# Down products with the activations stationary, and down weights staged a round ahead and copied by ScalarE, in a two-layer hybrid decoder trunk on one Trainium2 core

## The chip, the core and the metric

The kernel runs on one core of a Trainium2 chip. All times are microseconds (us) of device time for one execution, unless marked ns. The engines are TensorE (PE: matrix products; PEld is its weight load), VectorE (DVE), ScalarE (ACT), GpSimd (POOL) and SyncE (SP), whose queue here issues all loads from memory. Lower time is better.

## The reference

The program is a trunk of two residual layers on 256 tokens of width 1024, all in float32. Each layer has three token mixers (a gated delta rule, an RWKV-7 mixer and stick-breaking attention), which are merged by gates and projected. Layer 0 then has a dense SwiGLU of width 2816, layer 1 a mixture of 8 experts of width 3584 of which each token uses two. The mixture is what most of the change touches:

```
def swiglu(h, w_gate, w_up, w_down):
    return (jax.nn.silu(h @ w_gate) * (h @ w_up)) @ w_down

def moe_swiglu(h, router_w, w_gate, w_up, w_down):
    logits = (tokens @ router_w).astype(jnp.float32)
    top_vals, top_idx = lax.top_k(logits, TOP_K)
    top_w = jax.nn.softmax(top_vals, axis=-1)
    combine = jnp.sum(jax.nn.one_hot(top_idx, N_EXPERTS) * top_w[..., None], axis=1)
    for e in range(N_EXPERTS):
        y = swiglu(tokens, w_gate[e], w_up[e], w_down[e])
        out = out + combine[:, e:e + 1] * y
```

Reshapes and the token mixers are left out here.

## The kernel before, in words

Every engine runs its own program in its own order. They meet at semaphores: an instruction adds to one, another engine waits for a value. Nothing is scheduled by a planner; the order is that of the code.

**The expert stage** (`experts` on TensorE and VectorE, the loop at the end of the ScalarE program, and the loads at the end of the SyncE program) works in passes. A pass takes one expert and up to CAP = 80 of its tokens; there are eight passes in the profiled run. At its end a pass gathers the 80 tokens of the next one into xgT (products of the normed activations with a selection matrix). It then has NR = 4 rounds of FB = 7 tiles of 128 hidden columns each. A round on TensorE is:

- `hidden()`: gate and up products. The weights of the round lie in eight hidden slots (2 x 896 columns each). The weight tile is the stationary operand and the 80 tokens are the moving one. `columns_mm` splits each 128-column stationary tile in two halves of 64 columns, which write to the two halves of the output partitions. A semaphore (hid_used) frees each slot as soon as its products are done.
- ScalarE takes silu of the gate part (L1584 for four tiles, L1587 for three), VectorE multiplies with the up part into heT (128 hidden rows x 80 tokens for each of the 7 tiles).
- `down(0)` and `down(1)`: the products with the down weights, for the first four and the last three tiles. Again the weights are stationary, in halves of 64 columns, and heT moves; the result yT, 1024 outputs x 80 tokens, is summed in two banks of PSUM over all four rounds. The down weights of a round lie in three down slots (two, two and three tiles), freed by dwn_used (after `down(0)`) and dwn_mm.

At the end of a pass ScalarE copies yT out of PSUM (L1592), TensorE transposes it to 80 tokens x 1024 (L1292), ScalarE copies it again (L1596), and TensorE scatters it to all 256 tokens with the weighted selection matrix (L1299); VectorE adds that to x (L2032).

SyncE loads the eight hidden slots and then the three down slots of the following round, each after the semaphore that frees it. One hidden slot is 896 KB, the down slots are 1024, 1024 and 1536 KB. The first round's weights are loaded before the stage begins.

**Other places that the change touches.** At the start of each layer VectorE scales the activations of both token halves (`scaled`) and writes them transposed (`turned`) for TensorE's first products (L636). In `attention`, TensorE fills the waits between the attention products with pieces of the gate projections (`some(steps, 5)`, each piece being 2 products); a projection writes to one of two banks, and can only begin when VectorE has copied the one before last out of its bank (`opened`, L1876). In the dense SwiGLU the last three down tiles are kept back and done for one half of the tokens after the other.

The two lines of the code below that matter most are the products of `down` before:

```
ins = columns_mm(B[4 + half], slice(k % 4 * CAP, (k % 4 + 1) * CAP),
                 down_slot(n)[:, at, k * P:(k + 1) * P], heT[:, f, :], start=False, stop=False)
```

The functions that the change touches, with the line numbers of the profile:

Of the kernel before, what the change touches and what calls it, by code (L numbers as in the profile page):

```python
# [12 lines left out]
P = 128  # L13
D = 1024
# [5 lines left out]
DEPTH = 2  # L20
# [47 lines left out]
def build(nc, a, out):  # L68
    ctx = ExitStack()
    with ctx:  # L70
# [41 lines left out]
        eps_c = sb("eps_c", [P, 4])  # L112
        zeros = sb("zeros", [P, 4 * CAP], mybir.dt.bfloat16)
        stat = sb("stat", [P, 64])
# [19 lines left out]

        def down_slot(n):

            lo = 2 * KH * HSLOT
            return pool[:, lo + 2 * n * D:lo + min(2 * n + (3 if n == 2 else 2), FB) * D].rearrange("p (f n) -> p f n", n=D)

        assert 2 * KH * HSLOT + FB * D <= MRING * SLOT  # L140

# [80 lines left out]
        heT = region(FB * CAP).rearrange("p (j n) -> p j n", j=FB)  # L222
        yT = region(KD * CAP).rearrange("p (k n) -> p k n", k=KD)
        sge = region(FB * CAP).rearrange("p (j n) -> p j n", j=FB)
# [212 lines left out]
        he_silu, he_ready, hid_mm, dwn_mm = ff_silu.handle, ff_ready.handle, proj_mm.handle, down_mm.handle  # L437
        yT_ready = sem("yT_ready")
        ye_mm = sem("ye_mm")
        ye_ready = sem("ye_ready")  # L440
# [152 lines left out]
        def _(pe):  # L593
# [422 lines left out]
            def attention(l, steps):  # L1016
# [79 lines left out]
            def dense_ffn(l):  # L1096
# [39 lines left out]
                for c, (g, u, d) in list(enumerate(L[l]["ffn"]))[1:]:  # L1136
                    arrived(g)
                    arrived(u)
                    for i in range(2):
                        f = 2 * c + i  # L1140
                        ff_ready.wait(pe, 0, f - 1)
                        for s, w in ((0, weights(g)), (1, weights(u))):
                            for k in range(KD):
                                ins = mm(proj[f % 2][:, s * T:(s + 1) * T], w[:, k, i * P:(i + 1) * P], hnT[:, k, :],  # L1144
                                         start=(k == 0), stop=(k == KD - 1))
                        ff_mm.by(ins)

# [62 lines left out]
            def experts():  # L1210
# [7 lines left out]
                with pe.Fori(0, n_pass) as i:  # L1218
                    pe.wait_ge(xg_ready, i * 2 + 2)
                    pe.wait_ge(selT_ready, i + 1)  # L1220
                    for half in range(2):
                        mm(B[4 + half][:, 0:4 * CAP], zeros[:, 0:P], zeros[:, :], start=True, stop=False,
                           skip_group_check=True)
                    with pe.Fori(0, NR) as j:
# [38 lines left out]
                        def down(g):  # L1263

                            pe.wait_ge(he_ready, i * (2 * NR) + j * 2 + (ff_base + g + 3))
                            for f in groups[g]:
                                n, at = min(f // 2, 2), f - 2 * min(f // 2, 2)
                                if at == 0:
                                    pe.wait_ge(dwn_loaded[n],
                                               i * (16 * NR) + j * 16 + 16 * (slot_count[2 * KH + n] + 1))  # L1270
# [55 lines left out]
        def _(act):  # L1326
# [238 lines left out]
            for l in range(DEPTH):  # L1565
# [14 lines left out]
            n_pass = act.value_load(pass_expert[0:1, 0:1], min_val=MIN_PASSES, max_val=MAX_PASSES)  # L1580
            with act.Fori(0, n_pass) as i:
                for r in range(NR):
# [24 lines left out]
        def _(v):  # L1607
# [299 lines left out]
            def dense_ffn(l):  # L1907
# [3 lines left out]
                for t in range(NT):  # L1911
                    down_mm.wait(v, 0, down_mm.per_layer - 2 * (1 - t))
                    for half in range(2):
# [147 lines left out]
        def _(sp_):  # L2061
# [51 lines left out]
            def down_load(n, e, rows):  # L2113

                src = a["moe_w_down"][0, e, rows, :].rearrange("a (f p) n -> p (a f) n", p=P)
                sp_.dma_start(down_slot(n), src).then_inc(dwn_loaded[n], 16)  # L2116

# [12 lines left out]
            for ring in [None] + sorted(range(RING), key=lambda n: slot_last[n]):  # L2130
# [8 lines left out]
            assert len(fetched) == 2 * KH  # L2139

            sp_.wait_ge(passes_ready, 1)
            sp_.dma_start(fgain, a["final_norm_g"].partition_broadcast(P)).then_inc(fgain_loaded, 16)

            def later_round(e, col, hid, dwn):

                for n in range(2 * KH):
                    sp_.wait_ge(hid_used, hid + (n + 1))
                    hidden_load(n, bass.ds(e, 1), bass.ds(col, FB * P))
                for n in range(3):
                    if n < 2:  # L2150
                        sp_.wait_ge(dwn_used, dwn + 1)
                    else:
                        sp_.wait_ge(dwn_mm, dwn * 2 + (down_base + 2))
                    lo, size = down_rows(n)
                    down_load(n, bass.ds(e, 1), bass.ds(col + lo, size))

            def rest_of_pass(i, e):

                with sp_.Fori(0, NR - 1) as j:
                    later_round(e, j * (FB * P) + FB * P, i * (2 * KH * NR) + j * (2 * KH), i * NR + j)  # L2160

            more = sp_.value_load(pass_expert[0:1, MAX_PASSES + 1:MAX_PASSES + 2], min_val=MIN_PASSES - 1,
                                  max_val=MAX_PASSES - 1)
            with sp_.Fori(0, more) as i:
                e = sp_.value_load(pass_expert[0:1, bass.ds(i + 1, 1)], min_val=0, max_val=NE - 1)
                rest_of_pass(i, e)
                e = sp_.value_load(pass_expert[0:1, bass.ds(i + 2, 1)], min_val=0, max_val=NE - 1)
                later_round(e, 0, i * (2 * KH * NR) + (2 * KH * (NR - 1)), i * NR + (NR - 1))
            e = sp_.value_load(pass_expert[0:1, bass.ds(more + 1, 1)], min_val=0, max_val=NE - 1)
            rest_of_pass(more, e)  # L2170
            sp_.wait_ge(fin_ready, 1)
# [32 lines left out]
```

## Time and profile before

| what | value |
|---|---|
| median of three runs | 2055.0 us (2054.35 to 2058.61) |
| the profiled execution's own time | 2054.16 us |
| its span (first to last instruction) | 2052.4 us |
| TensorE busy | 1962.2 us (96%) |
| VectorE, ScalarE, GpSimd busy | 392.6, 271.1, 88.2 us |
| expert stage, from 1182 us to 2043 us | 861 us, TensorE busy 819.75 us, memory reads at 397 GB/s |
| dense SwiGLU, from 470 us to 696 us | 226 us, TensorE busy 225.66 us, 134 GB/s |
| mean granted TensorE clock, as a share of full speed | 0.984 |

The span lies 1.8 us under the time of its own execution, and that execution 0.8 us under the median. Busy time of TensorE is an upper bound on its work: products are pipelined, and their ends are modelled. A float32 product appears as two records (a MATMUL row with x64 stands for 32 products).

### The profile page before, as it was taken

Reading aid. Unit: us, or ns where it says so; the run is one execution under the profiler, and the core shown is the slowest. Engines: PE = TensorE matmul, PEld = TensorE weight load, DVE = VectorE, ACT = ScalarE, POOL = GpSimd, SP = SyncE. Lnnn points to the kernel's source line nnn. Section 1 sums busy time; section 2 is a strip of 40 time slices with the busy share of each in tenths; the row PEclk is TensorE's granted clock in tenths of the full one; section 3 lists DMA queues with packets and bytes.
Section 4 is the critical chain, followed back from the end, with each engine's and each line's share of the span. In section 5 each row is a group of like instructions: output and inputs, shape, how many; then the busy total and the mean of one; then the engine's idle time right before and its main releaser. Section 6 shows DMA issues by size and latency. Waiting matters only on the chain.

```text
span 2052.4 us, 66808 instructions
## 1 busy us (share of the span) xinstructions
PE 1962.2 (96%) x31214; PEld 1742.7 (85%) x31214; DVE 392.6 (19%) x948; ACT 271.1 (13%) x579; POOL 88.2 (4%) x174
## 2 busy tenths in 40 slices
PE   7999999999999999999999799999999999999997
PEld 7888887888777788888788799999999898989896
DVE  3335331110000133533211300101000101010001
ACT  1223223000000122222320000000000000000001
POOL 4011101000000001011000000000000000000000
PEclk9999999999999999999999899999999999999999
DMA  7313123467442151311345389999999999999996
GB/s 239 123 44 102 43 84 103 144 207 244 144 144 82 42 160 47 101 45 43 107 139 204 137 335 407 407 407 407 407 407 407 407 407 407 407 407 407 407 407 240
DMA packets 214760, 482.92 MB, mean 235 GB/s; under 512 B 11582, under 2 KB 110092, under 8 KB 214668
## 3 DMA queue, kind: packets, MB, share of 16 engines
q1 hardware_dynamic: 214668, 481.54, 62.9%
q8 instruction: 77, 1.26, 0.3%
q14 instruction: 15, 0.12, 0.0%
HBM read 480.46 MB, written 1.05 MB: 235 GB/s over the span
## 4 chain that ended last, share of the span: by engine, by line
PE 83%; DMA 6%; SPq 4%; DVE 3%; ACT 1%; issue 1%; POOL 0%; DVEq 0%; POOLq 0%
PE bank L1190 29%; PE bank L623 18%; PE bank L1144 7%; DMA pool<-in_moe_w_down_dram 6%; PE bank L713 5%; PE bank L1071 4%; PE bank L1104 4%; SPq L2111 3%; PE bank L1087 3%; PE bank L636 2%; PE bank L677 2%; PE bank L1299 1%; SPq L2116 1%; PE bank L1034 1%; DVE pool L1814 0%
## 5 line engine op out<-in xcount | busy, mean ns | idle before, releaser
L1190 PE MATMUL bank<-pool 128*64 128x80 f32 x21504 | 759.5, 234 | 32.1 <-DMA pool<-in_moe_w_down_dram 23.5
L1190 PEld LDWEIGHTS bank<-pool 128*64 128x64 f32 x21504 | 752.6, 138 | 40.3 <-DMA pool<-in_moe_w_down_dram 25.8
L623 PE MATMUL bank<-hnT,pool 128*128 128x256 f32 x1856 | 431.5, 386 | 6.4 <-DVE pool L1876 6.4
L623 PEld LDWEIGHTS bank<-hnT,pool 128*128 128x128 f32 x1856 | 349.0, 192 | 61.7 <-issue 14.4
L1144 PEld LDWEIGHTS bank<-hnT,pool 128*128 128x128 f32 x640 | 121.6, 190 | 24.6 <-issue 9.1
L1144 PE MATMUL bank<-hnT,pool 128*128 128x256 f32 x640 | 141.2, 379 | 0.0
L2019 DVE TENSOR_TENSOR pool<-pool,bank 128x320 f32<-128x320 f32 x32 | 15.6, 488 | 637.4 <-ACT pool L1584 637.4
L713 PEld LDWEIGHTS bank<-pool 64*64 64x64 f32 x3008 | 94.8, 135 | 17.2 <-issue 11.3
L713 PE MATMUL bank<-pool 64*64 64x32 f32 (+2 forms) x3008 | 103.4, 221 | 2.6 <-DVE pool L1660 1.6
L1584 ACT ACTIVATE pool<-bank 128x320 f32<-128x320 f32 x32 | 14.0, 437 | 675.5 <-PE bank L1190 675.5
L561 POOL TENSOR_TENSOR pool<-pool,level_mask 128x256 f32<-128x256 f32 x72 | 51.9, 736 | 782.1 <-DVE pool L1736 502.1
L1071 PE MATMUL bank<-oT,pool 128*128 128x256 f32 x384 | 85.4, 380 | 0.0
L1071 PEld LDWEIGHTS bank<-oT,pool 128*128 128x128 f32 x384 | 72.8, 190 | 10.2 <-issue 0.3
L1104 PE MATMUL bank<-pool 128*128 128x512 f32 x176 | 78.8, 592 | 0.0
L1104 PEld LDWEIGHTS bank<-pool 128*128 128x128 f32 x176 | 33.4, 190 | 33.5 <-issue 27.7
L1087 PE MATMUL bank<-pool 128*128 128x256 f32 x256 | 55.9, 379 | 0.0
L1087 PEld LDWEIGHTS bank<-pool 128*128 128x128 f32 x256 | 48.5, 190 | 6.5
L636 PE MATMUL bank<-hnT,pool 128*128 128x128 f32 x384 | 47.9, 290 | 4.6 <-DVE hnT L1631 4.6
L636 PEld LDWEIGHTS bank<-hnT,pool 128*128 128x128 f32 x384 | 47.3, 206 | 5.1 <-issue 5.0
L1910 DVE TENSOR_TENSOR pool<-pool,bank 128x256 f32<-128x256 f32 x22 | 9.3, 421 | 204.8 <-ACT pool L1562 204.8
L1660 DVE TENSOR_TENSOR pool<-pool,bank 128x128 f32<-128x128 f32 x108 | 26.7, 285 | 92.5 <-PE bank L713 92.5
L1562 ACT ACTIVATE pool<-bank 128x256 f32<-128x256 f32 x22 | 8.4, 383 | 206.8 <-PE bank L1144 195.7
(323 smaller groups left out, 1222.4 us busy)
## 6 DMA issues: line engine op xcount, KB each, us to landing
pool<-in_moe_w_up_dram SPq DMA_DIRECT2D x128, 896.0 KB, 16.6
pool<-in_moe_w_gate_dram SPq DMA_DIRECT2D x128, 896.0 KB, 16.6
pool<-in_w_in_dram SPq DMA_DIRECT2D x66, 1024.0 KB, 5.3
pool<-in_moe_w_down_dram SPq DMA_DIRECT2D x64, 1024.0 KB, 16.8
pool<-in_moe_w_down_dram SPq DMA_DIRECT2D x32, 1536.0 KB, 18.6
pool<-in_ffn_w_gate_dram SPq DMA_DIRECT2D x11, 1024.0 KB, 8.5
pool<-in_ffn_w_up_dram SPq DMA_DIRECT2D x11, 1024.0 KB, 5.7
pool<-in_ffn_w_down_dram SPq DMA_DIRECT2D x11, 1024.0 KB, 5.1
```

Of the source, the lines that this page charges most:

```text
L561: ml_ready.by(gp.tensor_tensor(Ml[:, 4 * g:4 * g + 4, :], m_of(g), rep(level_mask[:, b, :], 4), ALU.mult))
L623: ins = mm(ps[:, s * T:(s + 1) * T], w[:, k, (j + s) * P:(j + s + 1) * P], hnT[:, k, :], start=(k == 0), stop=(k == KD - 1))
L636: ins = mm(ps[:, s * T + t * P:s * T + (t + 1) * P], w(s, k), hnT[:, k, t * P:(t + 1) * P], start=(k == 0), stop=(k == KD - 1))
L677: ins = mm(ps[:, half * SW:(half + 1) * SW], hnT[:, k, t * P:(t + 1) * P], weights(n)[:, k, :], start=(k == 0), stop=(k == KD - 1))
L713: ins = mm(out(rows), lhs(rows), rhs(rows), start=True, stop=True, skip_group_check=True)
L1071: ins = mm(ps[:, s * T:(s + 1) * T], weights(n)[:, k, (j0 + s) * P:(j0 + s + 1) * P], oT[:, m // 4, k, :], start=(k == 0), stop=(k == GH - 1))
L1087: ins = mm(bank[:, s * SW:(s + 1) * SW], mT[:, k, t * P:(t + 1) * P], weights(n)[:, k, :], start=(k == 0), stop=(k == KD - 1))
L1104: ins = mm(B[2 * t + half][:, :], ffT[:, f, t * P:(t + 1) * P], weights(n)[:, i, half * 512:half * 512 + 512], start=(f == 0), stop=(f == ...
L1144: ins = mm(proj[f % 2][:, s * T:(s + 1) * T], w[:, k, i * P:(i + 1) * P], hnT[:, k, :], start=(k == 0), stop=(k == KD - 1))
L1190: ins = mm(bank[rows, cs], w[:, rows], rhs, start=start, stop=stop, skip_group_check=True)
L1660: ins = tt(old, old, part(B[2 + g][:, k * T:(k + 1) * T]), ALU.subtract)
L2111: sp_.dma_start(hidden_slot(n), src).then_inc(hid_loaded[n], 16)
```

## The change

It has one large part, in the expert stage, and three small ones.

1. **Down products.** heT (128 x 80) becomes the stationary operand and the down weights move, 512 columns at a time. The result is 80 tokens x 1024 outputs, so the transposes at the end of a pass and one of the two copies go away. `columns_mm` is not used for them any more.
2. **Down weights.** SyncE loads them into a stage (copy 0) a round ahead, ScalarE copies them from the stage into the slots that TensorE reads (copy 1). The stage takes the place of the former down slots, the slots are new. ScalarE's copies wait for the load and for TensorE's last read of the slot; SyncE's loads wait for ScalarE's copy.
3. **Small parts.** In `attention` TensorE's second filling has 4 pieces and not 5, and VectorE copies gate block 0 out after the first two heads and not after four. In the dense SwiGLU six down tiles are kept back and not three. At a layer's start VectorE writes the first half transposed before it scales the second.

```
@@ the stage and the slots
+        def down_tiles(n, copy):
+            lo = 2 * KH * HSLOT + copy * FB * D
+            return pool[:, lo + 2 * n * D:lo + min(2 * n + (3 if n == 2 else 2), FB) * D]
...
@@ TensorE, down(g)
-                                    for k in range(4 * half, 4 * half + 4):
-                                        ins = columns_mm(B[4 + half], slice(k % 4 * CAP, (k % 4 + 1) * CAP),
-                                                         down_slot(n)[:, at, k * P:(k + 1) * P], heT[:, f, :],
-                                                         start=False, stop=False)
+                                    ins = mm(B[4 + half][0:CAP, :], heT[:, f, :],
+                                             down_slot(n)[:, at, half * 512:half * 512 + 512], start=False, stop=False,
+                                             skip_group_check=True)
...
@@ TensorE, end of a pass
-                    for half in range(2):
-                        pe.wait_ge(yT_ready, i * 2 + (half + 1))
-                        for k in range(4):
-                            ins = pe.transpose(B[2 + half][0:CAP, k * P:(k + 1) * P], yT[:, 4 * half + k, :], ident[:])
-                        ins.then_inc(ye_mm, 1)
...
@@ ScalarE
+            def down_copy(n):
+                A(down_tiles(n, 1), down_tiles(n, 0), ACT.Copy).then_inc(dwn_ready, 1)
+
+            for n in range(3):
+                act.wait_ge(dwn_loaded[n], 16 * (slot_count[2 * KH + n] + 1))
+                down_copy(n)
...
+            def next_down(i, r, n):
+
+                act.wait_ge(dwn_loaded[n], i * (16 * NR) + 16 * (slot_count[2 * KH + n] + r + 2))
+                if n < 2:
+                    act.wait_ge(dwn_used, i * NR + (r + 1))
+                else:
+                    act.wait_ge(dwn_mm, i * (2 * NR) + (2 * r + down_base + 2))
+                down_copy(n)
...
+                    if not last or r < NR - 1:
+                        next_down(i, r, 0)
+                        next_down(i, r, 1)
+                        if r < NR - 1:
+                            next_down(i, r, 2)
...
-                    A(yT[:, 4 * half:4 * half + 4, :], B[4 + half][:, 0:4 * CAP].rearrange("p (k n) -> p k n", k=4),
-                      ACT.Copy).then_inc(yT_ready, 1)
-                for half in range(2):
-                    act.wait_ge(ye_mm, i * 2 + (half + 1))
-                    A(ye[0:CAP, half * 512:half * 512 + 512], B[2 + half][0:CAP, :], ACT.Copy).then_inc(ye_ready, 1)
+                    A(ye[0:CAP, half * 512:half * 512 + 512], B[4 + half][0:CAP, :], ACT.Copy).then_inc(ye_ready, 1)
+                if not last:
+                    next_down(i, NR - 1, 2)
...
@@ SyncE: in each round hidden slots of the next round, then the stage of the one after it
+            def down_round(i, r, e):
+
                 for n in range(3):
+                    sp_.wait_ge(dwn_ready, i * (3 * NR) + (3 * r + 3 + dwn_base + n + 1))
                     lo, size = down_rows(n)
+                    lo += (r + 2) % NR * FB * P
+                    down_load(n, e, slice(lo, lo + size))
...
@@ small parts
-                    some(steps, 5)
+                    some(steps, 4)
                     values(j)
...
-                opens = ((), (0, 1), (2,), (3,))
+                opens = ((0,), (1,), (2,), (3,))
...
-                        if f - 1 >= LAST - 2:
+                        if f - 1 >= LAST - 5:
...
+                v.wait_ge(vec_ready, l + 1)
+                turned(l, 0, 0)
                 scaled(l, 0, 1)
-                v.wait_ge(vec_ready, l + 1)
-                for t in range(NT):
-                    turned(l, 0, t)
+                turned(l, 0, 1)
```

How the order of instructions moves is shown at three places. The first is TensorE's round in the expert stage: the end of the hidden products and both down groups, before the change (one product is one row count here; L1190 is the line of `columns_mm`).

```order
L1190 MATMUL bank<-pool 64x80 x136
L1239 REGISTER_ALU
L1190 MATMUL bank<-pool 64x80 x56
L1265 REGISTER_ALU
L1269 REGISTER_ALU
L1190 MATMUL bank<-pool 64x80 x64
L1265 REGISTER_ALU
L1190 MATMUL bank<-pool 64x80 x48
L1224 REGISTER_ALU
```

And with the change (L1192 is `columns_mm`, L1275 the new product):

```order
L1192 MATMUL bank<-pool 64x80 x136
L1241 REGISTER_ALU
L1192 MATMUL bank<-pool 64x80 x56
L1267 REGISTER_ALU
L1271 ISA
L1271 REGISTER_ALU
L1275 MATMUL bank<-pool 80x512 x8
L1267 REGISTER_ALU
L1271 REGISTER_ALU
L1275 MATMUL bank<-pool 80x512 x6
```

The 64 + 48 down products of 64 output rows by 80 columns have become 8 + 6 of 80 rows by 512; the hidden products (32 more stand ahead of these rows) are as they were.

The second place is ScalarE between two rounds of a pass, before the change: the two silu of one round (L1584, L1587) and of the next.

```order
L1584 ACTIVATE pool<-bank 128x320
L1586 REGISTER_ALU
L1587 ACTIVATE pool<-bank 128x240
L1583 REGISTER_ALU
L1584 ACTIVATE pool<-bank 128x320
```

With the change (L1596, L1599 are the silu, L1573 the copies of the stage):

```order
L1596 ACTIVATE pool<-bank 128x320
L1598 REGISTER_ALU
L1599 ACTIVATE pool<-bank 128x240
L1586 REGISTER_ALU
L1588 REGISTER_ALU
L1573 ACTIVATE pool<-pool 128x2048 x2
L1590 REGISTER_ALU
L1573 ACTIVATE pool<-pool 128x3072
L1595 REGISTER_ALU
L1596 ACTIVATE pool<-bank 128x320
```

Three copies, of 2048, 2048 and 3072 elements a partition, now stand between the silu of one round and those of the next.

The third place is VectorE at the start of layer 0, before the change: L1625 is `scaled`, L2039 copies the vectors, L1631 is `turned` (two rows for each half of the tokens).

```order
L1625 TENSOR_SCALAR hn<-x,stat 128x1024
L2039 COPY vecs<-bank 128x103
L1625 TENSOR_SCALAR hn<-x,stat 128x1024
L1631 TENSOR_TENSOR hnT<-bank,vecs 128x4x128 x4
L1674 MEMSET pool 128x4x4
```

With the change (L1644, L2058 and L1650 are the same three):

```order
L1644 TENSOR_SCALAR hn<-x,stat 128x1024
L2058 COPY vecs<-bank 128x103
L1650 TENSOR_TENSOR hnT<-bank,vecs 128x4x128 x2
L1644 TENSOR_SCALAR hn<-x,stat 128x1024
L1650 TENSOR_TENSOR hnT<-bank,vecs 128x4x128 x2
```

The second `scaled` has moved behind the first half's two `turned` instructions.

## Rows read from the trace of the kernel before

**Rows 1.** Windows: length, PE, PEld, DVE, ACT, POOL busy, clock, DMA share, GB/s
```profile
480.00:685.00 205.00, 205.00 (x810) 152.14 (x810) 8.43 (x20) 7.66 (x20) 0.00 (x0) 1.00 0.38 126
1290.00:1398.00 108.00, 103.56 (x2779) 99.93 (x2777) 9.98 (x26) 6.46 (x13) 0.00 (x0) 0.98 1.03 407
```

**Rows 2.** Page, part 6: issues, KB each, us from issue to landing
```profile
pool<-in_moe_w_up_dram SPq DMA_DIRECT2D x128, 896.0 KB, 16.6
...
pool<-in_moe_w_down_dram SPq DMA_DIRECT2D x64, 1024.0 KB, 16.8
pool<-in_moe_w_down_dram SPq DMA_DIRECT2D x32, 1536.0 KB, 18.6
```

**Rows 3.** Waits from 1200 us to the end: us in total, times, longest
```profile
PE bank L1190 <- DMA pool<-in_moe_w_down_dram: 23.5, 14, 2.1
...
PE bank L1190 <- DMA pool<-in_moe_w_up_dram: 5.3, 6, 0.9
```

**Rows 4.** Windows: one round, from silu to silu
```profile
1224.09:1247.52 23.43, 23.43 (x679) 23.30 (x676) 3.24 (x13) 0.81 (x3) 0.00 (x0) 1.00 1.03 406
```

**Rows 5.** The chain that ended last, dense SwiGLU: start, us, what
```profile
492.33 3.43 PE bank L1104 x8
...
685.36 10.31 PE bank L1104 x24
```

**Rows 6.** Timeline at a pass's end: start, us, engine, operation, count, idle before
```profile
1280.04 2.39 PE L1190 MATMUL bank<-pool,hn 128*64 128x80 f32 x64
...
1282.36 1.07 PE L1292 MATMUL bank<-ident,pool 128*80 128x128 f32 x8
1282.47 0.49 DVE L2000 TENSOR_TENSOR pool<-bank,vecs 128x320 f32<-128x320 f32 x1 [0.61 <-PE bank L1190]
...
1283.77 3.67 PE L1299 MATMUL bank<-hnT,pool 80*128 80x512 f32 x8 [0.34 <-ACT hnT L1596]
...
1288.56 0.45 PE L1222 MATMUL bank<-zeros 128*128 128x320 bf16 x2 [0.89 <-DVE pool L2006]
...
1288.99 3.19 PE L1190 MATMUL bank<-pool 128*64 128x80 f32 x86
```

**Rows 7.** The chain, first pass of the expert stage
```profile
1182.64 9.49 PE bank L1190 x268
1192.13 0.21 issue
...
1196.99 1.83 issue
...
1208.49 0.67 issue
```

**Rows 8.** Timeline, attention of layer 0
```profile
308.60 0.56 DVE L1867 SCALAR_TENSOR_TENSOR pool<-bank,pool 128x384 f32<-128x384 f32 x1 [0.93 <-ACT pool L1531]
...
312.05 1.28 DVE L1876 COPY pool<-bank 128x512 f32<-128x512 f32 x2
...
312.88 1.19 PE L623 MATMUL bank<-hnT,pool 128*128 128x256 f32 x4 [3.20 <-DVE pool L1876]
```

**Rows 9.** Timeline, start of layer 1
```profile
699.23 0.74 DVE L1625 TENSOR_SCALAR hn<-x,stat 128x1024 f32<-128x1024 f32 x1
...
701.31 3.97 PE L636 MATMUL bank<-hnT,pool 128*128 128x128 f32 x17 [2.31 <-DVE hnT L1631]
```

**Rows 10.** Groups of ScalarE: count, busy, mean ns, idle before
```profile
L1405 ACT ACTIVATE pool<-pool 128x2048 f32<-128x2048 f32 x2 | 3.8, 1901 | 0.0
```

**Rows 11.** Timeline of ScalarE ahead of the expert stage
```profile
1159.24 0.20 ACT L1354 ACTIVATE stat<-stat 128x1 f32<-128x1 f32 x1
...
1169.47 0.20 ACT L1578 ACTIVATE pool<-pool 128x2 f32<-128x2 f32 x1 [10.03 <-DVE pool L1943]
```

**Rows 12.** Windows, ahead of the expert stage
```profile
1166.00:1170.00 4.00, 1.11 (x6) 1.01 (x6) 2.58 (x16) 0.20 (x1) 0.00 (x0) 0.50 0.00 0
```

**Rows 13.** Timeline, scatter of the last pass
```profile
2039.19 3.67 PE L1299 MATMUL bank<-hnT,pool 80*128 80x512 f32 x8 [0.34 <-ACT hnT L1596]
```

More of the change, by code:

```diff
@@ L112, in build @@
         eps_c = sb("eps_c", [P, 4])
-        zeros = sb("zeros", [P, 4 * CAP], mybir.dt.bfloat16)
+        zeros = sb("zeros", [P, 512], mybir.dt.bfloat16)
         stat = sb("stat", [P, 64])
@@ L133, in hidden_slot, with down_slot @@
             return pool[:, n * HSLOT:(n + 1) * HSLOT].rearrange("p (k n) -> p k n", k=2)
[L135 to L140, printed above, removed]
+        def down_tiles(n, copy):
+            lo = 2 * KH * HSLOT + copy * FB * D
+            return pool[:, lo + 2 * n * D:lo + min(2 * n + (3 if n == 2 else 2), FB) * D]
+        def down_slot(n, copy=1):
+            return down_tiles(n, copy).rearrange("p (f n) -> p f n", n=D)
+        assert 2 * KH * HSLOT + 2 * FB * D <= MRING * SLOT
         banks = [ctx.enter_context(nc.psum_tensor(f"bank{i}", [P, 512], F32)) for i in range(8)]
@@ L222, in build @@
         heT = region(FB * CAP).rearrange("p (j n) -> p j n", j=FB)
-        yT = region(KD * CAP).rearrange("p (k n) -> p k n", k=KD)
         sge = region(FB * CAP).rearrange("p (j n) -> p j n", j=FB)
@@ L437, in build @@
         he_silu, he_ready, hid_mm, dwn_mm = ff_silu.handle, ff_ready.handle, proj_mm.handle, down_mm.handle
-        yT_ready = sem("yT_ready")
-        ye_mm = sem("ye_mm")
+        dwn_ready, dwn_base = yrs_ready.handle, DEPTH * yrs_ready.per_layer
         ye_ready = sem("ye_ready")
@@ L1221, in experts @@
                     for half in range(2):
-                        mm(B[4 + half][:, 0:4 * CAP], zeros[:, 0:P], zeros[:, :], start=True, stop=False,
+                        mm(B[4 + half][0:CAP, :], zeros[:, 0:CAP], zeros[:, :], start=True, stop=False,
                            skip_group_check=True)
@@ L1268, in down @@
                                 if at == 0:
-                                    pe.wait_ge(dwn_loaded[n],
-                                               i * (16 * NR) + j * 16 + 16 * (slot_count[2 * KH + n] + 1))
+                                    pe.wait_ge(dwn_ready, i * (3 * NR) + j * 3 + (dwn_base + n + 1))
                             for half in range(2):
@@ L1579, in _, with one_pass @@
             act.wait_ge(passes_ready, 1)
-            n_pass = act.value_load(pass_expert[0:1, 0:1], min_val=MIN_PASSES, max_val=MAX_PASSES)
-            with act.Fori(0, n_pass) as i:
+            more = act.value_load(pass_expert[0:1, MAX_PASSES + 1:MAX_PASSES + 2], min_val=MIN_PASSES - 1,
+                                  max_val=MAX_PASSES - 1)
+            def next_down(i, r, n):
[5 more added lines that the diff above has]
+                down_copy(n)
+            def one_pass(i, last):
                 for r in range(NR):
@@ L1588, in _ @@
                       ACT.Silu).then_inc(he_silu, 1)
+                    if not last or r < NR - 1:
[3 more added lines that the diff above has]
+                            next_down(i, r, 2)
                 for half in range(2):
                     act.wait_ge(dwn_mm, i * (2 * NR) + (down_base + 2 * NR - 1 + half))
-                    A(yT[:, 4 * half:4 * half + 4, :], B[4 + half][:, 0:4 * CAP].rearrange("p (k n) -> p k n", k=4),
-                      ACT.Copy).then_inc(yT_ready, 1)
-                for half in range(2):
-                    act.wait_ge(ye_mm, i * 2 + (half + 1))
-                    A(ye[0:CAP, half * 512:half * 512 + 512], B[2 + half][0:CAP, :], ACT.Copy).then_inc(ye_ready, 1)
+                    A(ye[0:CAP, half * 512:half * 512 + 512], B[4 + half][0:CAP, :], ACT.Copy).then_inc(ye_ready, 1)
+                if not last:
+                    next_down(i, NR - 1, 2)
+            with act.Fori(0, more) as i:
+                one_pass(i, False)
+            one_pass(more, True)
             ln_exp_tables()
@@ L1911, in dense_ffn @@
                 for t in range(NT):
-                    down_mm.wait(v, 0, down_mm.per_layer - 2 * (1 - t))
+                    down_mm.wait(v, 0, down_mm.per_layer - 3 * (1 - t))
                     for half in range(2):
@@ L2115, in down_load @@
                 src = a["moe_w_down"][0, e, rows, :].rearrange("a (f p) n -> p (a f) n", p=P)
-                sp_.dma_start(down_slot(n), src).then_inc(dwn_loaded[n], 16)
+                sp_.dma_start(down_slot(n, 0), src).then_inc(dwn_loaded[n], 16)
             def down_rows(n):
@@ L2139, in _, with hidden_round @@
             assert len(fetched) == 2 * KH
+            for n in range(3):
+                sp_.wait_ge(dwn_ready, dwn_base + n + 1)
+                lo, size = down_rows(n)
+                down_load(n, slice(0, 1), slice(FB * P + lo, FB * P + lo + size))
             sp_.wait_ge(passes_ready, 1)
             sp_.dma_start(fgain, a["final_norm_g"].partition_broadcast(P)).then_inc(fgain_loaded, 16)
-            def later_round(e, col, hid, dwn):
+            def hidden_round(i, r, e):
+                col = (r + 1) % NR * FB * P
                 for n in range(2 * KH):
-                    sp_.wait_ge(hid_used, hid + (n + 1))
-                    hidden_load(n, bass.ds(e, 1), bass.ds(col, FB * P))
+                    sp_.wait_ge(hid_used, i * (2 * KH * NR) + (2 * KH * r + n + 1))
+                    hidden_load(n, e, slice(col, col + FB * P))
+            def down_round(i, r, e):
                 for n in range(3):
[L2150 to L2153, printed above, removed]
+                    sp_.wait_ge(dwn_ready, i * (3 * NR) + (3 * r + 3 + dwn_base + n + 1))
                     lo, size = down_rows(n)
[L2155 to L2160, printed above, removed]
+                    lo += (r + 2) % NR * FB * P
+                    down_load(n, e, slice(lo, lo + size))
             more = sp_.value_load(pass_expert[0:1, MAX_PASSES + 1:MAX_PASSES + 2], min_val=MIN_PASSES - 1,
@@ L2165, in _ @@
                 e = sp_.value_load(pass_expert[0:1, bass.ds(i + 1, 1)], min_val=0, max_val=NE - 1)
-                rest_of_pass(i, e)
+                e = bass.ds(e, 1)
+                for r in range(NR - 2):
+                    hidden_round(i, r, e)
+                    down_round(i, r, e)
+                hidden_round(i, NR - 2, e)
                 e = sp_.value_load(pass_expert[0:1, bass.ds(i + 2, 1)], min_val=0, max_val=NE - 1)
-                later_round(e, 0, i * (2 * KH * NR) + (2 * KH * (NR - 1)), i * NR + (NR - 1))
+                e = bass.ds(e, 1)
+                down_round(i, NR - 2, e)
+                hidden_round(i, NR - 1, e)
+                down_round(i, NR - 1, e)
             e = sp_.value_load(pass_expert[0:1, bass.ds(more + 1, 1)], min_val=0, max_val=NE - 1)
-            rest_of_pass(more, e)
+            e = bass.ds(e, 1)
+            hidden_round(more, 0, e)
+            down_round(more, 0, e)
+            hidden_round(more, 1, e)
+            hidden_round(more, 2, e)
+            down_round(more, 1, e)
             sp_.wait_ge(fin_ready, 1)
```

## The prediction, made before the changed kernel ran

> **What bounds the kernel now.** I read the windows by stage first. In the expert stage two limits lie close together: a pass takes 108 us, the memory reads run at 407 GB/s with the DMA engines' share at 1.03, and TensorE is busy for 103.56 of the 108 us [rows 1]. The sizes of the loads say which one binds: a round reads 8 x 896 + 2 x 1024 + 1536 KB = 11.01 MB [rows 2] (gate loads have the size of up loads), which at 407 GB/s is 27.05 us, so four rounds are 108.2 us. That is the pass. Before, memory sets the time of seven of the eight passes. The view of waits says how near TensorE is: it waits for down and up weights 23.5 + 5.3 = 28.8 us in the whole stage [rows 3], 3.6 us a pass. So TensorE has 3.6 us to spare in each pass and not more. That number decides the case, since the change alters the cost of a third of TensorE's products there.
>
> A round without waits takes TensorE 23.43 us [rows 4] for 224 hidden and 112 down products of 64 x 80, so 69.7 ns each: 15.62 us hidden, 7.81 us down.
>
> **The change part by part.**
>
> *Down products.* A round has 7 tiles x 2 halves = 14 products with 512 moving columns. The nearest row is the dense SwiGLU's, the same type and the same 512 columns, weights moving: 3.43 us for 4 products (8 records), 10.31 us for 12 [rows 5], so 0.859 us each, in a stretch where TensorE was busy for all of 205 us [rows 1]. 14 x 0.859 = 12.03 us in place of 7.81: **4.22 us more in each round**. Its stationary tile has 128 columns, the new one 80. From below: if the cost went by the filled output positions, 80 of 128, a product would cost 0.537 us and a round 7.5 us. From above stands the scatter: 4 products (8 records) of 512 columns over only 80 rows of the array took 3.67 us, 0.92 each [rows 6], with the last one's drain in it; 14 of those are 12.9 us, and the stage would take 27 us more than by 0.859. I take 0.859: the row that shares the length of the moving operand in an unbroken run. The scatter also speaks against the low value, since a part-filled array was not faster there.
>
> Why the old form was cheap can be read from the same rows: 69.7 ns for 80 columns in a 64-column half, two of which make the 128 columns of a tile, so 139 ns a tile, while 80/512 of 859 ns is 134 ns for a whole tile. The halves run side by side. The new form fills 80 of 128 output columns for its whole length. That is the loss: 128/80 = 1.6, less the small overhead of short products.
>
> The Trainium skill says this too, in TensorEngine Tiling, When to Use Tiling: swapping stationary and moving operand gains column tiling only where the operand that becomes stationary has a free size of at most 64. Here it has 80, so the swap gives up a tiling and gets none. The trace's 69.7 against 859 ns agrees, as far as the rows go.
>
> *The end of a pass.* Before, 1280.04 (gather) to 1288.99 (next round) is 8.95 us [rows 6]. The transposes L1292 and the first copy go; the scatter at 1283.77 then waits only for the second multiply of the gathered tokens, which ends at 1282.96 [rows 6], because the new copies of 80 x 512 run under the gather (the first half of the down sum is complete three products earlier, the second needs one copy, and the gather lasts 2.39 us). Scatter about 1283.07: 0.7 us gained. The zeroing product has 512 columns in place of 320, 0.45 us for two now [rows 6]: 0.2 us lost. 8.45 us.
>
> *A pass on TensorE* is 4 x (15.62 + 12.03) + 8.45 = **119.05 us**, over the 108.2 us that memory needs. TensorE becomes the limit, and the 28.8 us of waits vanish into it.
>
> *The stage and the copies.* A copy of 2048 elements a partition is 1.90 us on ScalarE [rows 10], one of 3072 by that 2.85, together 6.65 us a round; none is on the path. ScalarE idles more than 20 us of each round before (0.81 us busy of 23.43, [rows 4]). Copies 0 and 1 can begin when `down(0)` is done and end 3.8 us later, at about the end of `down(1)` (6 x 0.859 = 5.2 us); copy 2 ends 2.9 us into the next round, and the next silu comes after some 14 us of hidden products. What stands behind a waiting copy on ScalarE is that silu: if a stage load were late by more than about 11 us, TensorE would wait. It is not, as loads need 27.05 of a round's 27.65 us and catch up by 8.45 us at each pass's end. What was late before, the last down slot (freed only at the end of its round), is now hidden by the stage. But TensorE's wait for it was the 3.6 us spare, which is already counted.
>
> The first copies stand ahead of the exponential of the routing: ScalarE ends the norm at 1159.4 and is wanted at 1169.47 [rows 11], 6.65 us of copies fit. The loads of the first stage (9 us) go into a stretch where the DMA engines stand still [rows 12]; this helps a memory-bound stage and is worth nothing to one that TensorE binds.
>
> *Small parts.* In attention TensorE waits 3.20 us for VectorE's copy at 312.05 [rows 8]. The copy of block 0 alone can follow the multiply-add that ends at 309.16: TensorE resumes about 2.9 us earlier. The piece taken out of the second filling is done in the last filling, which has room for it, so it costs nothing. Twice, for two layers: 5.8 us. At a layer's start one `scaled` of 0.74 us leaves the path to L636 [rows 9]: 0.7 us a layer, 1.4. Six kept tiles and not three: the same products on the same engine, and VectorE's norm of the next layer still waits for both halves, so nothing. Together 7.2 us.
>
> **The sum**, against the profiled execution's 2054.2 us. Before, from the first product of the expert stage to the end of the last scatter: 1182.64 [rows 7] to 2042.86 [rows 13], 860.2 us. After: 8 x 119.05 = 952.4, less the 1.55 us of a pass's end that lie behind the scatter, plus the gaps of the first pass (four of them, 3.2 us in all; the first, the longest and the last are in [rows 7]) = 954.0 us. So +93.8 - 7.2 = +86.6: 2140.8 us for this execution; the median stands 0.8 us above it. I say **2140 us**, rounded down, since the first gaps may shrink when the loads come sooner.
>
> **Rivals.**
>
> *A, the other side: the long products are cheaper than the dense SwiGLU shows, and the stage stays bound by memory.* It decides at the product's price p where 4 x (15.62 + 14p) + 8.45 equals 108.2 us, p = 0.665 us; with the 7.2 us and the 9 us of early loads (2.0 us a pass) no loss remains up to 0.70 us. For p = 0.54, the low bound: 2054.2 - 7.2 - 9.0, plus about 2 us as the last load is followed by a copy before its products, = 2040 us. For it: only that no row shows 80 columns stationary with 128 rows. Against it: both rows with 512 moving columns lie at 0.86 to 0.92 us. Chance 0.04.
>
> The Trainium skill has a figure that would give this case: TensorE: Matmul & The Clock Gate, Back-to-back issue gap, gives about 131 ns for each 512-column product in a real stream, and about 216 ns for one by the simple formula. An estimate by that page, four times 131 ns for float32, is 0.52 us a product, and the stage would stay at the memory's pace. The trace is against it: 859 ns is four times 215 ns.
>
> *B: TensorE also waits, because the queues hold each other.* SyncE loads in one order: the third stage load waits for ScalarE's copy 2, which ends 2.9 us into the round, and the hidden loads stand behind it. If the DMA engines stood still for those 2.9 us in each round, a round would need 27.05 + 2.9 = 29.95 us and a pass 119.8, above 119.05: 8 x 0.8 = 6 us more; with a second wait of the same size for `down(0)`'s end, 8 x 3 = 24 us. For it: the copies, in-order queues, and a margin of only 0.6 us in a round. Against: hidden slots are only freed from some 3.6 us on, so the queue has work from before. 2146 to 2165 us, chance 0.09.
>
> *C: the small parts give nothing* (the attention is limited by ScalarE's chain right behind the wait): +7.2 us, 2147. It lies in the range and is part of the forecast's own chance.
>
> **How the numbers follow.** Forecast (TensorE-bound at 0.859 us a product) 0.85, its own range 2128 to 2150 (0.02 us a product is 14 x 32 x 0.02 = 9 us; small parts 0 to 8 us). A 0.04, B 0.09, and 0.02 for a price between. The range 2126 to 2158 leaves out A and the upper half of B, and of the high bound of 0.92 us (2167) it reaches two thirds. A measurement tells 0.2%, some 4 us, from no change: faster 0.03, within it 0.01, slower 0.96.
>
> **What would show it.** A new group with 512 columns, 448 products (896 records), near 385 us in all, in the place of a third of L1190's 759 us. Passes of 119 us at some 370 GB/s, no waits of TensorE for DMA, TensorE busy through. ScalarE with 96 copies, 1.9 and 2.9 us. The 3.2 us gap in the attention gone. I am wrong if the new products take 0.7 us or less, if passes stay at 108 us, or if TensorE waits for the copies.

## The result, and the profile after

The changed kernel takes **2143.2 us** (median of 4 runs, 2141.39 to 2144.91), the kernel before in the same comparison 2056.11 us. The ratio is 1.0423, with a 95% interval of 1.0404 to 1.0441: slower by 87 us, where 85 us were forecast (2140 against 2055). The profiled execution took 2144.91 us, where the prediction's sum gave 2140.8; its span is 2143.2 us.

The page's groups show where the time went. Columns as in part 5: line, engine, operation, tiles, count, busy us, mean ns, idle before and what ended it. L1192 is `columns_mm`, L1275 the new down product, L1573 ScalarE's copies. The first row is the same group in the kernel before.

```profile
L1190 PE MATMUL bank<-pool 128*64 128x80 f32 x21504 | 759.5, 234 | 32.1 <-DMA pool<-in_moe_w_down_dram 23.5
...
L1192 PE MATMUL bank<-pool 128*64 128x80 f32 x14336 | 503.3, 233 | 1.9 <-issue 1.9
...
L1275 PE MATMUL bank<-pool 128*80 128x512 f32 x896 | 391.8, 594 | 0.0
...
L1573 ACT ACTIVATE pool<-pool 128x2048 f32<-128x2048 f32 (+1 forms) x96 | 207.1, 2188 | 245.8 <-PE bank L1275 232.4
```

L1190's 759.5 us of before have become 503.3 + 391.8 = 895.1 us: 136 us more work for TensorE. The time rose by less, since in each pass some of the new work fills time in which TensorE waited for weights before [rows 3]. Now its idle time ahead of these products is 1.9 us in the whole stage, and none of it is for DMA. The chain that ended last shows a pass from the start of its rounds to the start of the next, in order of time (start us, us, what):

```profile
1297.18 15.64 PE bank L1192 x448
1312.83 12.17 PE bank L1275 x28
1325.00 15.64 PE bank L1192 x448
1340.64 12.17 PE bank L1275 x28
1352.82 15.64 PE bank L1192 x448
1368.46 12.17 PE bank L1275 x28
1380.64 15.65 PE bank L1192 x448
1396.28 12.17 PE bank L1275 x28
1408.46 2.39 PE bank L1192 x64
...
1411.49 3.71 PE bank L1294 x8
...
1416.92 3.12 PE bank L1192 x85
```

A round is 15.64 + 12.17 us without a gap, the end of a pass (gather at 1408.46 to the next round at 1416.92) 8.46 us, the pass 119.74 us. The windows of two passes answer to [rows 1] (length, busy time of PE, PEld, DVE, ACT, POOL, clock, DMA share, GB/s):

```profile
1297.00:1417.00 120.00, 118.44 (x1985) 82.93 (x1986) 9.97 (x26) 31.38 (x23) 0.00 (x0) 1.00 0.95 368
1417.00:1536.00 119.00, 117.47 (x1978) 82.48 (x1976) 9.97 (x26) 31.38 (x23) 0.00 (x0) 1.00 0.95 368
```

The memory reads have fallen from 407 to 368 GB/s: TensorE is now the slower of the two. Note how little PE's busy share tells: 96% in the window of before, 99% in these, and the limit has changed from one resource to the other.

### The profile page after: what moved, and what is told of

Read it like the earlier page. It is cut to its first block, busy times and chain, and to the rows that moved or that the text cites. A ratio compares the mean times of both kernels' runs of the same rounds, so it can differ in the third digit from the quotient of the medians.

```text
span 2143.2 us, 54280 instructions
## 1 busy us (share of the span) xinstructions
PE 2088.4 (97%) x24878; PEld 1615.0 (75%) x24878; DVE 392.5 (18%) x948; ACT 469.4 (22%) x658; POOL 88.4 (4%) x174
## 4 chain that ended last, share of the span: by engine, by line
PE 94%; DVE 3%; ACT 1%; issue 1%; DMA 0%; SPq 0%; POOL 0%; DVEq 0%
PE bank L1192 24%; PE bank L1275 18%; PE bank L625 18%; PE bank L1146 6%; PE bank L715 5%; PE bank L1073 4%; PE bank L1106 4%; PE bank L1089 3%; PE bank L638 2%; PE bank L679 1%; PE bank L1294 1%; PE bank L1036 0%; DVE pool L1833 0%; PE bank L770 0%; PE bank L996 0%
## 5 line engine op out<-in xcount | busy, mean ns | idle before, releaser
L1192 PEld LDWEIGHTS bank<-pool 128*64 128x64 f32 x14336 | 497.9, 137 | 24.6 <-issue 24.6
L1192 PE MATMUL bank<-pool 128*64 128x80 f32 x14336 | 503.3, 233 | 1.9 <-issue 1.9
L1275 PE MATMUL bank<-pool 128*80 128x512 f32 x896 | 391.8, 594 | 0.0
L625 PEld LDWEIGHTS bank<-hnT,pool 128*128 128x128 f32 x1856 | 349.5, 192 | 56.0 <-issue 8.5
L1275 PEld LDWEIGHTS bank<-pool 128*80 128x80 f32 x896 | 131.8, 150 | 235.2 <-issue 232.3
L1573 ACT ACTIVATE pool<-pool 128x2048 f32<-128x2048 f32 (+1 forms) x96 | 207.1, 2188 | 245.8 <-PE bank L1275 232.4
L1146 PEld LDWEIGHTS bank<-hnT,pool 128*128 128x128 f32 x640 | 121.6, 190 | 23.4 <-issue 7.6
L715 PEld LDWEIGHTS bank<-pool 64*64 64x64 f32 x3008 | 94.8, 135 | 17.3 <-issue 11.3
L1596 ACT ACTIVATE pool<-bank 128x320 f32<-128x320 f32 x32 | 14.0, 437 | 408.8 <-PE bank L1192 408.8
## 6 DMA issues: line engine op xcount, KB each, us to landing
pool<-in_moe_w_up_dram SPq DMA_DIRECT2D x128, 896.0 KB, 10.5
```

The source lines that it names most:

```text
L625: ins = mm(ps[:, s * T:(s + 1) * T], w[:, k, (j + s) * P:(j + s + 1) * P], hnT[:, k, :], start=(k == 0), stop=(k == KD - 1))
L715: ins = mm(out(rows), lhs(rows), rhs(rows), start=True, stop=True, skip_group_check=True)
L1192: ins = mm(bank[rows, cs], w[:, rows], rhs, start=start, stop=stop, skip_group_check=True)
L1275: ins = mm(B[4 + half][0:CAP, :], heT[:, f, :], down_slot(n)[:, at, half * 512:half * 512 + 512], start=False, stop=False, skip_group_chec ...
L1573: A(down_tiles(n, 1), down_tiles(n, 0), ACT.Copy).then_inc(dwn_ready, 1)
```

## The experiments

All times are medians, ratios against the kernel before on the same chip, with 95% intervals. The kernel before had a median of 2056.4 us beside experiments 1 to 4 and of 2055.8 us beside the others.

**1. The old products, with all the rest of the change.** In `down`, at the pass's end and in ScalarE's copies there:

```
-  ins = mm(B[4 + half][0:CAP, :], heT[:, f, :], down_slot(n)[:, at, half * 512:half * 512 + 512], ...)
+  for k in range(4 * half, 4 * half + 4):
+      ins = columns_mm(B[4 + half], slice(k % 4 * CAP, (k % 4 + 1) * CAP),
+                       down_slot(n)[:, at, k * P:(k + 1) * P], heT[:, f, :], ...)
```

> The changed kernel with one thing undone: the down products have the weights stationary again, in halves of 64 columns, with the transposes and both copies at a pass's end. The stage, ScalarE's copies, SyncE's order and the small parts stay. My theory (the long products alone make it slower, TensorE is the limit there): TensorE needs 4 x 23.44 + 8.95 = 102.7 us a pass, memory 108.2, so passes of 108 us again, the 9 us of early loads and the 7.5 us of the small parts show, and the time is 2036 to 2046 us, faster than before. Rival (ScalarE's copies and the queues that hold each other cost something of their own): TensorE waits for copies, 2056 us or more.

Measured: 2046.6 us, ratio 0.9952 (0.9935 to 0.9969). Undoing this one edit takes 96.6 us off and makes the kernel faster than before. So the long products alone are the loss. But it is 0.6 us above my range, and its median lies 4 us above that of experiment 3, which has no stage (the two intervals overlap). ScalarE's timeline in the last round shows a loss there, and experiment 7 tests it (start, duration, [idle before]):

```profile
2010.04 1.91 ACT L1582 ACTIVATE pool<-pool 128x2048 f32<-128x2048 f32 x1 [17.30 <-DMA pool<-in_moe_w_down_dram]
2012.51 1.91 ACT L1582 ACTIVATE pool<-pool 128x2048 f32<-128x2048 f32 x1 [0.56 <-DMA pool<-in_moe_w_down_dram]
2016.35 2.76 ACT L1582 ACTIVATE pool<-pool 128x3072 f32<-128x3072 f32 x1 [1.93 <-DMA pool<-in_moe_w_down_dram]
2019.02 0.42 ACT L1605 ACTIVATE pool<-bank 128x320 f32<-128x320 f32 x1
...
2020.25 10.01 PE L1195 MATMUL bank<-pool 128*64 128x80 f32 x224 [4.61 <-DVE pool L2051]
```

In the last pass the last stage loads stand behind all hidden loads, so they are not a round ahead any more: SyncE's code for that pass issues the hidden loads of the last two rounds and only then the last stage loads. ScalarE waits 17.3 us for them with the silu queued behind; TensorE waits 4.6 us and then needs 10.01 us for down products that took 7.8 us in the round of [rows 4]. The granted clock in the window from 2020 to 2025 us was 0.55, near the lower of the two levels, 1.2 GHz, after a stretch in which TensorE was mostly idle (0.64 of 5 us busy from 2015 to 2020 us).

**2. The new products without the stage.** The kernel before with the new `down`, the shorter pass end and the small parts; the loads go straight to the slots, ScalarE copies nothing.

> The kernel before with the new down products and the small parts, without the stage: loads go straight to the slots, ScalarE copies nothing. My theory: TensorE binds, so the stage is worth nothing to it, passes of 119.7 us, 2140 to 2146 us. Rival (the stage is what keeps the loads ahead, as a round has only 0.8 us more than its loads need): TensorE waits for the last down slot, some 2 us in each of 32 rounds, 2170 to 2210 us. Second rival (copies slow TensorE's products down): below 2135 us.

Measured: 2142.5 us, ratio 1.0419 (1.0401 to 1.0436), the same as the changed kernel. The chain shows the same rounds:

```profile
1415.91 15.64 PE bank L1188 x448
1431.55 12.17 PE bank L1272 x28
```

The stage and its 96 copies neither cost nor gain anything where TensorE binds. Both rivals of this run are out.

**3. The small parts alone**, on the kernel before:

```
-                    some(steps, 5)
+                    some(steps, 4)          # the second filling
-                opens = ((), (0, 1), (2,), (3,))
+                opens = ((0,), (1,), (2,), (3,))
```

with the six kept tiles and `turned` ahead of the second `scaled`, as in the diff above.

> The kernel before with the small parts alone: VectorE's earlier copy in attention, four pieces in the second filling, six down tiles kept back in the dense part, the first half written transposed before the second is scaled. My theory: 2.9 us a layer in attention and 0.7 us a layer at the start, 2048 to 2050 us. Rival (they only shift waits): 2054 to 2057 us.

Measured: 2042.4 us, ratio 0.9938 (0.9922 to 0.9955): 14 us faster by the medians, 9 to 16 us by the interval, where I had worked out 7.2. The two profiled executions lie 11.6 us apart (spans of 2040.8 and 2052.4 us). The chain of the attention in layer 0, from VectorE's copy on:

```profile
308.55 0.61 DVE pool L1876
309.16 0.14 issue
309.29 1.10 PE bank L623 x4
310.39 0.65 PE bank L1034 x2
311.04 0.22 PE bank L1035 x2
311.26 0.65 PE bank L1034 x2
```

and the same place in the kernel before:

```profile
312.13 0.61 DVE pool L1876
312.88 1.19 PE bank L623 x4
314.07 1.28 PE bank L1034 x2
315.35 0.43 PE bank L1035 x2
315.77 1.28 PE bank L1034 x2
```

After its wait of 3.2 us [rows 8] TensorE ran the same products in twice the time: each L1034 row, one product, took 1.28 us and not 0.65. The windows of before give the clock there:

```profile
312.00:314.00 2.00, 1.12 (x5) 1.01 (x6) 1.33 (x3) 0.00 (x0) 0.41 (x1) 0.94 1.02 388
314.00:316.00 2.00, 2.00 (x6) 1.30 (x5) 0.00 (x0) 0.19 (x1) 0.00 (x0) 0.50 0.01 3
316.00:318.00 2.00, 2.00 (x8) 1.41 (x7) 0.00 (x0) 0.79 (x2) 0.42 (x2) 0.71 0.00 0
```

The clock is 0.50 from 314 to 316 us, which is 1.2 GHz, after an idle stretch; without the wait it stays at 1.00. The wait cost 3.0 us by itself, the slow products 1.7 us, and some 0.3 us is left for the end of the attention, where TensorE no longer waits for the last chain of ScalarE and GpSimd: 5.0 us for this attention, where I had counted 2.9.

**4. 64 stationary columns, in pairs.** The down products leave out tokens 64 to 79 of each pass, and the second half of the outputs stays in the upper 64 partitions, where they are not copied out whole:

```
...
+  for half in range(2):
+      ins = mm(B[4 + half][64 * half:64 * half + 64, :], heT[:, f, 0:64],
+               down_slot(n)[:, at, half * 512:half * 512 + 512], ...)
```

> The changed kernel with 64 stationary columns in place of 80: the down products leave out tokens 64 to 79 of a pass, and the two output halves of a tile go to the two column halves of the array, one behind the other. The rest is as changed. If two 64-column products of 512 run side by side, a pair costs about 0.87 us, a round 6.1 us and TensorE needs 4 x 21.8 + 8.5 = 95.5 us a pass: bound by memory again, 2034 to 2046 us. If only the moving columns count and nothing runs side by side, it costs what 80 columns do: 2140 to 2146 us.

Measured: 2044.1 us, ratio 0.9938 (0.9921 to 0.9955). The same number of products with the same 512 moving columns:

```profile
L1275 PE MATMUL bank<-pool 128*64 128x512 f32 x896 | 200.4, 599 | 6.5 <-DVE pool L2038 6.5
```

200.4 us in place of 391.8, 0.895 us for a pair on average over the stage. The chain shows a round's down part in a pass:

```profile
1368.67 6.01 PE bank L1275 x28
```

That is 14 products in 6.01 us, 0.859 us for a pair, less than a single product of 80 columns takes (0.869). So two products run side by side in the two column halves. The stage is bound by memory again: the same part of the next pass begins at 1476.93, 108.3 us later, at 407 GB/s, and TensorE waits for gate and up weights. The form "activations stationary" is not dear in itself; 80 columns are: each of these products has TensorE for itself for 0.869 us and fills 80 of 128 columns. The 6.5 us of idle time in the row above are one wait in the last round, of the kind of experiment 1.

**5 and 6. Fewer moving columns.** The changed kernel with 448 and with 384 moving columns in each down product, which leaves out 128 and 256 of the 1024 outputs:

```
-  ins = mm(B[4 + half][0:CAP, :], heT[:, f, :], down_slot(n)[:, at, half * 512:half * 512 + 512], ...)
+  ins = mm(B[4 + half][0:CAP, 0:448], heT[:, f, :], down_slot(n)[:, at, half * 512:half * 512 + 448], ...)
```

> The changed kernel with 448 moving columns in each down product in place of 512 (it leaves out 128 of the 1024 outputs). All the rest is as changed. If the product's price goes by its moving columns, 0.869 x 448/512 = 0.760 us, a round is 15.64 + 10.65 us and a pass 4 x 26.29 + 8.46 = 113.6 us, still over the memory's 108.2: 8 x 6.1 us less than the changed kernel, 2094 us. If something else had set the 119.7 us, the time moves less than that.

> The same with 384 moving columns (it leaves out 256 of the 1024 outputs): 0.652 us a product, just under the 0.665 us at which the passes of TensorE and of memory are equal. A round is 24.77 us and a pass 107.5 us, so memory takes over at 108.2: 2050 to 2060 us with ScalarE's block in the last round, which cost the run with the old products some 7 us. If the price alone counted, without a floor, the next step from 448 columns would be as large as the last; memory's floor takes about 0.7 us of it in each pass.

Measured: 2095.1 us (ratio 1.0196, 1.0177 to 1.0214) and 2047.5 us (0.9958, 0.9943 to 0.9973). In the chain the down part of a round:

```profile
1417.97 10.68 PE bank L1275 x28
```

with 448 columns, and with 384:

```profile
1416.30 15.64 PE bank L1192 x448
1431.94 9.19 PE bank L1275 x28
```

So 0.869, 0.763 and 0.656 us for 512, 448 and 384 columns: 0.0017 us a column, straight. The time follows, -48.1 and then -47.6 us a step. I had expected the last step to end at memory's floor and to be smaller for it. It is not: the pass takes 4 x 24.83 + 8.46 = 107.8 us, which is TensorE's sum, 0.4 us under the 108.2 that the loads need, and TensorE waits for no load in the whole stage. The memory reads are at 407 GB/s, their rate of before, with TensorE busy 98.44 of 100 us, so the two limits are very close; 8 x 0.4 us is less than the 9 us of early loads and need not show. The time lies 2.5 us below my range. ScalarE's wait in the last round, 12.9 us, did not reach TensorE in this run. The two runs show that the price goes by the moving columns and that the time follows it down to 0.656 us. The price at which memory takes over, 0.665 us by the prediction, they do not show; the floor itself shows in experiment 4, whose passes take 108.3 us with much cheaper products.

**7. The third copy of the last round behind the silu**, in the kernel of experiment 1:

```
-                        if r < NR - 1:
+                        if r < NR - 1 and not (last and r == NR - 2):
                             next_down(i, r, 2)
+                    if last and r == NR - 1:
+                        next_down(i, NR - 2, 2)
```

> The run with the old products and the stage, with one more thing: in the last round the third copy stands behind the two silu and not ahead of them. In the run before, ScalarE waited there for the last loads with the silu queued behind it; TensorE waited 4.6 us and then ran at the lower clock. My theory: TensorE goes on at once, 6 to 7 us less, 2039 to 2041 us, the fastest so far. Rival (the last loads themselves are late): under 2 us less, about 2045 us.

Measured: 2040.8 us, ratio 0.9928 (0.9910 to 0.9945), 5.8 us less than experiment 1 by the two medians, and the times of the two kernels do not touch (2039.4 to 2041.7 against 2045.6 to 2048.8 us). ScalarE and TensorE in the last round:

```profile
1989.81 32.70 PE L1195 MATMUL bank<-pool 128*64 128x80 f32 x934
...
2013.31 0.42 ACT L1605 ACTIVATE pool<-bank 128x320 f32<-128x320 f32 x1
...
2015.36 2.77 ACT L1582 ACTIVATE pool<-pool 128x3072 f32<-128x3072 f32 x1 [0.33 <-DMA pool<-in_moe_w_down_dram]
```

The silu comes at 2013.31 with the third copy behind it, and TensorE goes through the round and the down products in one stretch of 32.7 us. It is the lowest median of all, but its interval overlaps that of experiment 3: against the small parts alone the stage's gain is not shown. One trace of each points to some gain: from the first product of the expert stage to the end of the last scatter are 859.1 us in experiment 3 (1172.16 to 2031.27) and 855.0 us here (1174.77 to 2029.75), where the prediction had put the early loads at 9 us for a stage bound by memory.

**8. The attention edits alone**, on the kernel before.

> The kernel before with the attention edits alone: the earlier copy on VectorE, and four pieces in TensorE's second filling. The trace of the small parts shows 5.0 us less in each attention, of which I had foreseen 2.9. If the attention edits are the cause, 9 to 12 us less than the kernel before, 2044 to 2047 us. If the order at a layer's start or the dense part gives the surplus, 6 us less, 2050 us.

Measured: 2045.4 us, ratio 0.9948 (0.9929 to 0.9968), 10.3 us less. The two attentions are 10 of the 14 us of experiment 3. The intervals of the two runs overlap, so a rest for the other small parts isn't shown by the times. The traces say more. The six kept tiles give nothing: in experiment 3 the dense part's first products begin 5.62 us ahead of before (461.02 against 466.64) and those after its last norm 5.61 us (692.21 against 697.82). At the start of the expert stage experiment 3 is 10.5 us ahead of before (1172.16 against 1182.64) and this run 9.0 us (1173.62). That difference arises early in layer 0: at 304 us, ahead of the first attention, experiment 3 is 0.6 us ahead of before and this run 1.9 us behind it. In the window from 78 to 90 us the granted clock was 0.86 in experiment 3, as in before, and 0.72 here. This run's edits lie in the attention alone and cannot be what put it behind. So no gain of the other small parts is shown beyond the half us at a layer's start; the rest of the 3.7 us between the medians may be the clock.

## Why the prediction was right, step by step

- **"Before, memory sets the time"**: right. With the old products (experiments 1, 3, 7) the stage stays at the memory's pace, 407 GB/s, with the new ones (2) it does not, stage or no stage. The prediction's "3.6 us to spare and not more" was too little, though. By its own terms a pass needs 4 x 23.43 + 8.95 = 102.7 us on TensorE, so 108.2 leaves 5.5; the list of waits for weights shows only part of the slack. The sum used 108.2 and 119.05 and was not touched by this.
- **The product's price, 0.859 us**: measured 12.17/14 = 0.869 us, so 4.38 us more in a round (15.64 + 12.17 against 23.43) and not 4.22. This is the term that was off: 12.17 against 12.03 us, 32 times, is 4.5 us, and the stage took 958.5 us (1175.10 to 2133.63) where I had 954.0. Why 80 stationary columns cost 0.01 us more than the dense part's 128 I did not test. The choice between the bounds was right, and experiments 5 and 6 show that the moving columns set the price.
- **The loss of the side-by-side halves**: shown by experiment 4, 0.859 us a pair against 2 x 0.869. The rule of the Trainium skill, TensorEngine Tiling (Array Packing), When to Use Tiling (the swap gains column tiling for a free size up to 64), holds in both directions here: 64 gains the tiling, 80 does not. The figure of 131 ns of the Trainium skill, TensorE: Matmul & The Clock Gate, Back-to-back issue gap, does not hold for these float32 products: an estimate of four times it would be 0.52 us, and 0.869 was measured.
- **The end of a pass**: 8.45 forecast, 8.46 measured, by the two steps named: from gather to scatter 3.03 us and not 3.73, from there to the next round some 0.2 us more. **The pass**: 119.05 against 119.74 us. **The first gaps**: 1.9 us (0.35 and 1.55 in the chain) in place of 3.2.
- **The copies cost nothing**: right for this kernel (experiment 2), by the cover that I named. A loose end of rival B was there all the same: ScalarE, blocked by a late load with the silu behind it. It came with the last pass's order, and cost experiment 1 some 6 us. In the changed kernel ScalarE waited up to 10.8 us for such a load too, but TensorE did not wait for it.
- **The small parts, 7.2 us**: the total was right by luck, its parts were not. In the profile the expert stage begins 7.5 us earlier (1175.10 against 1182.64 in [rows 7]). But each attention gives 5.0 us, not 2.9, since I had not counted the slow clock after the wait. Against these 10 us stands a loss early in layer 0, where I had expected a gain of 0.7: the first products begin 0.74 us earlier (12.86 against 13.60) but take longer, so that the next ones are 0.64 us late at 20 us; in the window from 78 to 90 us the granted clock was 0.74 where before had 0.86; and at the first attention the changed kernel is 2.3 us behind. At the start of layer 1 the wait is 0.5 us shorter, not 0.7. Experiment 3 had 0.86 in that window and was 10.5 us ahead at the stage. No run here shows what moves the clock between these kernels.
- **Rival A** (cheaper products) and **B** (queues that hold each other up) did not come about, and in the attention C's opposite did.

## What to carry to other kernels

When two resources lie within a few per cent of each other, work out what each needs for one period (here 108.2 us of loads, 102.7 us of products) before trading one for the other: an edit that adds 17 us of products to each such period takes it to 119.7 us, whatever it does for the loads. The price of these float32 products went by their moving columns, whether they filled 80 or 128 stationary columns, so compare the two forms by moving columns and by whether two narrow tiles run side by side; two of 64 columns did, those of 80 did not. And if an engine in the middle of a chain is given copies that wait for loads, put them behind the work that others wait for, above all in the last round, where nothing is a round ahead any more. And before a few us between two kernels are given to an edit, look where in the traces they arise: experiment 8 was 1.9 us behind the kernel before ahead of everything that its edits touch.

## What the runs showed of the hardware beyond this

A wait of 3.2 us on TensorE was followed by some 4 us at a lower granted clock (0.50 in the window from 314 to 316 us, 0.71 in the next 2 us), in which two products took 1.28 us each and not 0.65. So the attention's wait cost 4.7 us, a half more than the trace's idle column says. The same happened in the last round of experiment 1, after a wait of 4.6 us. Copies of 128 x 2048 on ScalarE took 1.90 us and of 128 x 3072 2.76 us, and 96 of them beside TensorE's products changed those by nothing that can be measured (12.17 us for the down part with and without them).
